# U turned ahead of the first F group, more unread products in TensorE's waits, the last modulation block behind the output products, and branch sums in PSUM

## The chip, the cores and the metric

The kernel is one program for one core of a Trainium2 chip. The metric is the time of a launch on the device in microseconds (us). Engines are named as in the profile: TensorE (PE, and PEld for its loads of the stationary operand), VectorE (DVE), ScalarE (ACT), GpSimd (POOL), and SyncE (SP), which issues nearly all DMAs. Work is ordered between engines by semaphores: an instruction increments one (`then_inc`), another engine waits for a count (`wait_ge`). The page gives the clock that TensorE was granted in tenths of its full 2.4 GHz; its two levels are 1.2 and 2.4 GHz (0.50 and 1.00).

## The reference, cut to what matters

Two blocks run in series on 256 tokens of width 1024, in float32.

```python
# first block, one layer: an S5 state-space mixer, a squared-ReLU MLP, a gated embedding
h = rmsnorm(x, norm_mix)
bu = einsum('blgh,gph->blgp', h by 64 groups of 16, bb)      # complex, state 64 per group
xs = associative_scan(combine, (a, bu))                      # over the 256 tokens
y = gelu(real(xs, c) + d * h);  a, g = split(y @ w_glu);  x = x + a * sigmoid(g)
x = x + relu(rmsnorm(x) @ mlp_w1) ** 2 @ mlp_w2
x = rmsnorm(x + (p @ ple_w) * sigmoid(rmsnorm(x) @ ple_gate_w))
# second block, two layers, a stream x and a context stream ctx (256 tokens)
mod_x, mod_c = silu(c) @ w_ada + b_ada, silu(c_ctx) @ w_ada + b_ada     # 6 x 1024 each
px, pc = split(modulate(rms_norm(x)) @ w_in), split(modulate(rms_norm(ctx)) @ w_in)
y_four, y_conv = fft mixing @ w_four, depthwise conv + layer norm + silu @ w_conv
y_gqa, y_diff = grouped attention @ w_gqa, differential attention @ w_diff
x = x + g_m * (sum(sigmoid(gate_b) * y_b over the 4 branches) @ w_out)
x = x + g_f * swiglu(modulate(rms_norm(x)))                             # ctx too in layer 0
```

## The kernel before, in words

**Products.** A float32 operand is split into a high and a low part (`xh`/`xl`, `wh`/`wl`), and each product is three matmuls: high by high, low by high, high by low (`gemm_pe`, lines 2597 to 2599). Weights stream through a ring of four slots of 1 MB (`raw`), loaded by SP in the fixed order of a list; SP waits until the slot's last user is done. ScalarE makes the high half (`split_hi`, line 819), GpSimd the low half (line 2584; the first two GLU loads are done by VectorE, `gate_lo`, line 3081), and `w_ready` counts the halves. `wh` and `wl` hold two loads. PSUM is two tensors of four banks: `gb` for GEMMs, `mb` for the rest.

**The head** (the first 126 us) builds the state-space mixer as products over chunks of 8 tokens. TensorE runs, in this order: transposes of the lambdas; 21 products nobody reads (`warm`); the transposes of x; 64 transposes that turn x into U (line 2683, [32 x 128] each, into all of `mb`); two products for the row factors `fac` (2690); 8 transposes of c (2696); 4 of the vectors (2701); `warm(2, 2)`; a loop over 32 pairs of groups (2713 and 2724), with modulation blocks 0 to 3 between; the Toeplitz products (2748, 2775, 2761) and blocks 4 to 9; `warm(7, 1)`; then 8 times `y_products(d)` (2799, 2804), after each a late modulation block or one unread product. The late blocks follow y_products 0, 1, 3 and 6. Then GLU starts, first with three weight halves side by side over the eight operand tiles (`leading`).
VectorE computes the first F group (`f_group(0)`, with `mb[:, 0]` as scratch, hence TensorE's wait on `s_F` ahead of the transposes of U), the inverse norms, U itself (3013: `mb` times `fac`), F groups 1 to 3, part of E, the state scan S, the last part of E, `gate_lo` for GLU's load 0, and a loop over the 8 outputs, each turned out of PSUM (`turn_y`, 3090) and passed through the gelu with ScalarE; `gate_lo(1, 0)` and `gate_lo(1, 1)` are inside this loop, behind d = 1 and 3. ScalarE copies `fac` (2360), the row zero of F group 0, then C (2364, 2365), on which the vector transposes and GpSimd's E wait.
SP issues the first four loads when U is turned (`s_U`), the seven zero fills of the Toeplitz tile behind `s_ct5`, and the seven copies inside it (line 640) ahead of ring load 12. The load of the last late block takes the slot of GLU's load 1, so it waits for `gate_lo(1, 1)`.

**Modulation.** `ada_block(n)` (line 667) multiplies 256 columns of w_ada by silu(c) and silu(c_ctx): 8 products, `x16` in the trace, as every float32 product is two records.

**A layer** (`layer_pe`, `layer_act`, `layer_dve`) runs in-projections, Fourier mixing, branch 0, grouped attention, branch 2, diff attention, branches 1 and 3, the out-projection (`wo`), a norm and the feed-forward. Layer 0 has 512 tokens, layer 1 has 256. A branch has four pairs of 256 columns: a gate GEMM, for which ScalarE takes a tanh, and a branch GEMM. VectorE forms `prod = (tanh + 1) * product` (line 2165) and adds it into `mix` in SBUF (2167 to 2171). For branch 3 the result is halved and split again: high by ScalarE (`mixed_hi`, 1832), low by VectorE (`mixed_lo`, 2148), the operands of `wo`.
In the attention loops (`grouped_pe`, `diff_pe`) TensorE issues the scores of item i (1197 to 1201), the transposes of the probabilities of item i - 2 (1208), and the outputs of item i - 3.

**Norms.** `norm_pe` sums squares, and while VectorE forms the inverse root it runs modulation blocks and `unused_products`, products of 256 columns that nobody reads. Norm 7 is that of layer 1's feed-forward.

## Time and profile before

| | us |
|---|---|
| three runs | 1982.76, 1982.89, 1986.4; median 1982.89 |
| the profiled execution | 1981.52 |
| its span, first to last instruction | 1979.7 |
| TensorE busy | 1906.8 |
| GpSimd, VectorE, ScalarE busy | 1108.2, 932.6, 756.2 |
| DMA: bytes from HBM, share of 16 engines | 266.70 MB, 43.1% (queue q1) |
| mean granted clock of TensorE | 0.981 |

The page has the sums; where a stage waits is read from the views by time: stretches (busy time and clock of each engine in a window), the timeline (instructions in order, in brackets how long the engine was idle before and what released it), and the chain of waits. A matmul's duration in the timeline overlaps its neighbours'; for a run of them take the next start less the first.

### The profile page before, as it was taken

To read this page: it belongs to the slowest core of one execution; us is meant where nothing else is said; L and a number is where in the kernel's file an instruction comes from. 1 tells how busy PE (TensorE), PEld (TensorE's weight loads), DVE (VectorE), ACT (ScalarE), POOL (GpSimd) and SP (SyncE) were. 2 spreads that over 40 slices of the span, in tenths; PEclk is the share of its full clock that TensorE was granted. 3 is DMA by queue.
4 is the path that set the end of the run, shared out by engine and by line. 5 is a ranking of instruction groups with operands and counts; after the bars stand their busy time and mean duration, and the time that the engine had idled before them with its cause. 6 is when DMAs were issued, how large, how long until landed. Compare 5 with 4: busy or idle time off the path is not lost.

```text
span 1979.7 us, 31484 instructions
## 1 busy us (share of the span) xinstructions
PE 1906.8 (96%) x13077; PEld 1639.1 (83%) x13077; DVE 932.6 (47%) x1688; ACT 756.2 (38%) x1212; POOL 1108.2 (56%) x611
## 2 busy tenths in 40 slices
PE   8989999989999999999999999999999998989997
PEld 5578999877887788778878888888788987989997
DVE  7956542254935793752443111114476756382112
ACT  4343553333234523642323222222345536434443
POOL 6426898563535443334543444444368754868885
PEclk8989999989999999999999999999999999999999
DMA  6857766764222132114334323223535331665653
GB/s 167 239 200 238 262 216 213 263 202 161 64 74 86 33 123 69 33 65 138 107 109 147 92 84 119 89 75 105 190 125 156 119 106 43 213 227 174 195 168 99
DMA packets 289490, 276.60 MB, mean 140 GB/s; under 512 B 19802, under 2 KB 276324, under 8 KB 289092
## 3 DMA queue, kind: packets, MB, share of 16 engines
q1 hardware_dynamic: 286804, 271.42, 43.1%
q10 hardware_dynamic: 2192, 2.77, 0.5%
q8 instruction: 103, 1.69, 0.4%
q0 software_dynamic: 352, 0.40, 0.1%
q14 instruction: 39, 0.32, 0.0%
HBM read 266.70 MB, written 4.19 MB: 137 GB/s over the span
## 4 chain that ended last, share of the span: by engine, by line
PE 88%; DVE 5%; ACT 2%; DMA 2%; issue 1%; SPq 1%; POOL 1%; ACTq 0%; DVEq 0%; POOLq 0%
PE gb L2597 19%; PE gb L2599 19%; PE gb L2598 19%; PE gb L1755 3%; PE gb L1756 3%; PE gb L1754 3%; PE gb L1482 3%; PE gb L1484 3%; PE gb L1483 3%; PE mb L1208 1%; DMA raw<-in_w_ada 1%; PE gb L667 1%; PE mb L667 1%; PE mb L1275 1%; PE mb L1355 1%
## 5 line engine op out<-in xcount | busy, mean ns | idle before, releaser
L2584 POOL TENSOR_TENSOR wl<-raw,wh 128x1024 fp32r<-128x1024 f32 (+3 forms) x448 | 978.2, 2202 | 780.1 <-ACT wh L819 779.8
L819 ACT CAST wh<-raw 128x1024 fp32r<-128x1024 f32 (+3 forms) x452 | 420.2, 938 | 651.8 <-PE gb L2599 375.6
L2597 PE MATMUL gb<-xh,wh 128*128 128x256 f32 (+1 forms) x1856 | 602.5, 325 | 10.6 <-DVE xl L1158 5.3
L2598 PE MATMUL gb<-xl,wh 128*128 128x256 f32 (+1 forms) x1856 | 598.5, 322 | 0.0
L2599 PE MATMUL gb<-xh,wl 128*128 128x256 f32 (+1 forms) x1856 | 598.4, 322 | 0.0
L2597 PEld LDWEIGHTS gb<-xh,wh 128*128 128x128 f32 x1856 | 350.7, 189 | 46.9 <-issue 11.7
L2599 PEld LDWEIGHTS gb<-xh,wl 128*128 128x128 f32 x1856 | 350.7, 189 | 27.5
L2598 PEld LDWEIGHTS gb<-xl,wh 128*128 128x128 f32 x1856 | 350.9, 189 | 27.2
L1754 PE MATMUL gb<-fhh,wh 128*128 128x512 f32 (+1 forms) x352 | 118.4, 336 | 0.0
L1756 PE MATMUL gb<-fhh,wl 128*128 128x512 f32 (+1 forms) x352 | 117.9, 335 | 0.0
L1755 PE MATMUL gb<-fhl,wh 128*128 128x512 f32 (+1 forms) x352 | 117.9, 335 | 0.0
L1482 PE MATMUL gb<-wh,xh 128*128 128x512 f32 x272 | 107.5, 395 | 0.0
L2261 DVE SCALAR_TENSOR_TENSOR x<-gb,mod,x 128x256 f32<-128x256 f32 x72 | 31.9, 480 | 160.1 <-PE gb L1756 136.9
L1483 PE MATMUL gb<-wh,xl 128*128 128x512 f32 x272 | 105.9, 390 | 0.0
L1484 PE MATMUL gb<-wl,xh 128*128 128x512 f32 x272 | 105.9, 389 | 0.0
L2285 DVE SCALAR_TENSOR_TENSOR pr<-th,gb 128x1024 f32<-128x1024 f32 (+1 forms) x22 | 21.0, 955 | 138.2 <-ACT th L1890 138.2
L2599 PE MATMUL gb<-brh,wl 128*128 128x512 f32 (+1 forms) x256 | 85.8, 335 | 0.0
L2597 PE MATMUL gb<-brh,wh 128*128 128x512 f32 (+1 forms) x256 | 85.8, 335 | 0.0
L2598 PE MATMUL gb<-brl,wh 128*128 128x512 f32 (+1 forms) x256 | 85.7, 335 | 0.0
L2290 DVE TENSOR_TENSOR pr<-pr,gb 128x1024 f32<-128x1024 f32 (+1 forms) x22 | 21.0, 955 | 135.9 <-PE gb L2599 135.9
L2084 DVE SCALAR_TENSOR_TENSOR mb<-upad,vecs,mb 128x256 f32<-128x256 f32 (+1 forms) x152 | 79.5, 605 | 0.0
L867 ACT ACTIVATE th<-gb 128x512 f32<-128x512 f32 (+1 forms) x44 | 34.1, 774 | 115.7 <-PE gb L2599 115.7
(475 smaller groups left out, 3020.2 us busy)
## 6 DMA issues: line engine op xcount, KB each, us to landing
raw<-in_w_in SPq DMA_DIRECT2D x62, 1024.0 KB, 5.3
raw<-in_w_ada SPq DMA_DIRECT2D x48, 1024.0 KB, 5.5
raw<-in_w_ffn SPq DMA_DIRECT2D x44, 1024.0 KB, 5.2
raw<-in_mlp_w SPq DMA_DIRECT2D x32, 1024.0 KB, 5.6
raw<-in_w_ffn SPq DMA_DIRECT2D x16, 768.0 KB, 4.3
raw<-in_w_ffn SPq DMA_DIRECT2D x16, 640.0 KB, 4.1
raw<-in_ssm_w_glu SPq DMA_DIRECT2D x8, 1024.0 KB, 7.1
raw<-in_w_out SPq DMA_DIRECT2D x8, 1024.0 KB, 4.8
```

Source lines behind the costliest of these rows:

```text
L819: nc.scalar.copy(split_half(wh, p, j, h), raw_half(p, it, j, h)).then_inc(hi_ready, 1)
L1482: nc.tensor.matmul(g, xh[:, k, ts], H[:, kk], start=(k == 0), stop=False)
L1483: nc.tensor.matmul(g, xl[:, k, ts], H[:, kk], start=False, stop=False)
L1484: ins = nc.tensor.matmul(g, xh[:, k, ts], L[:, kk], start=False, stop=(k == KD - 1))
L1754: nc.tensor.matmul(o, H[:, kk, :], XH, start=(k == 0), stop=False)
L1755: nc.tensor.matmul(o, H[:, kk, :], XL, start=False, stop=False)
L1756: ins = nc.tensor.matmul(o, L[:, kk, :], XH, start=False, stop=(k == kt - 1))
L2084: D1.add(v.scalar_tensor_tensor(dst, u, w, src, ALU.mult, ALU.add))
L2584: nc.gpsimd.tensor_tensor(split_half(wl, p, j, h), raw_half(p, it, j, h), split_half(wh, p, j, h).bitcast(F32), ALU.subtract)\
L2597: nc.tensor.matmul(o, H[:, k, :], XH, start=st, stop=False)
L2598: nc.tensor.matmul(o, H[:, k, :], XL, start=False, stop=False)
L2599: return nc.tensor.matmul(o, L[:, k, :], XH, start=False, stop=sp_)
```

## The change

In the head, TensorE turns groups 16 to 63 of U before it waits for the first F group, and groups 0 to 15 after it. The 8 transposes of c move ahead of the two products for `fac`; ScalarE copies C before `fac` and row zero. `warm(7, 1)` becomes `warm(13, 1)`. The late modulation blocks follow y_products 0, 1, 3 and 7; behind the one at index 6 there is an unread product instead.
`unused_products` takes a place. Three stand behind the first scores of the grouped heads, four behind the third of the diff heads (both layers), and norm 7 has seven in place of two.
The products of branch 3 and their final sums with `mix` go to `mb` (`mixed_pair`), two banks per pair of tiles, and both splits read them there; VectorE waits on `s_ml` for the splits of two pairs before it reuses a bank. Branches 0 to 2, the running sums and the norm tiles stay in SBUF.

```diff
-        def unused_products(n):
+        def unused_products(n, place=None):
             for _ in range(n):
-                nc.tensor.matmul(gb[:, 2, 0:2 * P], ones[:, :], ...
+                nc.tensor.matmul(gb[:, 2, 0:2 * P] if place is None else place, ones[:, :], ...
@@ norm_pe
-                unused_products(2 if n == 7 else 1)
+                unused_products(7 if n == 7 else 1)
@@ grouped_pe, for i, ahead of the scores
+                    if i == 1:
+                        if c0 >= 4:
+                            pe.wait_ge(s_ex, c0 - 3)
+                        unused_products(3, gb[:, c0 % 4, 0:2 * P])
@@ diff_pe, behind the scores
                 if i == 2:
                     pe.wait_ge(s_qtl, TN[l, "d"] + 8)
                     pe.wait_ge(s_qv, l + 1)
+                    unused_products(4, mb[:, mine[0] % 2, 0:2 * P])
@@ layer_act, mixed_hi
-                    nc.scalar.mul((brh if k < 4 else xh)[:, k, home("layer", T)], mix[:, k, 0:T], 0.5).then_inc(s_mh, 1)
+                    nc.scalar.mul((brh if k < 4 else xh)[:, k, home("layer", T)], mixed_pair(l, k // 2)[:, k % 2, :], 0.5)\
+                        .then_inc(s_mh, 1)
+        def mixed_pair(l, pair):
+            return mb[:, 2 * (pair % 2):2 * (pair % 2) + 2, 0:layer_T(l)]
@@ layer_dve, mixed_lo
-                    v.scalar_tensor_tensor(lo[:, k, home("layer", T)], mix[:, k, 0:T], 0.5, ...
+                    v.scalar_tensor_tensor(lo[:, k, home("layer", T)], mixed_pair(l, k // 2)[:, k % 2, :], 0.5, ...
@@ branch_dve
+                        if b == 3 and pair > 1:
+                            dve.wait_ge(s_ml, 8 * l + 2 * (pair - 1))
-                        prod = dst if b == 0 else two(pr2, s_, T)
+                        prod = dst if b == 0 else mixed_pair(l, pair) if b == 3 else two(pr2, s_, T)
                         if b == 3:
-                            v.tensor_tensor(dst, dst, prod, ALU.add).then_inc(s_mx, 1)
+                            v.tensor_tensor(prod, dst, prod, ALU.add).then_inc(s_mx, 1)
@@ ScalarE, head: the copy of fac and f_row_zero(0) move behind the two copies of C
-            act.wait_ge(s_fp5, 1)
-            nc.scalar.copy(fac[:, :], gb[:, 3, 0:NCH]).then_inc(s_fac, 1)
-            f_row_zero(0)
             act.wait_ge(s_ct5, 1)
...
+            act.wait_ge(s_fp5, 1)
+            nc.scalar.copy(fac[:, :], gb[:, 3, 0:NCH]).then_inc(s_fac, 1)
+            f_row_zero(0)
@@ TensorE, head: and the two products for fac (s_fp5) move behind the transposes of c (s_ct5)
-            pe.wait_ge(s_F, 1)
             pe.wait_ge(s_xg, CH)
-            for g in range(GROUPS):
+            for g in (*range(16, GROUPS), *range(16)):
+                if g == 0:
+                    pe.wait_ge(s_F, 1)
...
-            warm(7, 1)
+            warm(13, 1)
...
-                late = ((0,), (1,), (), (2,), (), (), (3,), ())[d]
+                late = ((0,), (1,), (), (2,), (), (), (), (3,))[d]
```

## Rows read from the trace of the kernel before

**Rows 1.** The page, head and part 1: busy us (share of span) x instructions.

```profile
span 1979.7 us, 31484 instructions
...
PE 1906.8 (96%) x13077; PEld 1639.1 (83%) x13077; DVE 932.6 (47%) x1688; ACT 756.2 (38%) x1212; POOL 1108.2 (56%) x611
```

**Rows 2.** Stretches of 10 us: length, busy (instructions) per engine, granted clock, DMA share, GB/s.

```profile
20.00:30.00 10.00, 6.72 (x30) 3.76 (x29) 9.33 (x20) 8.69 (x10) 7.67 (x9) 0.94 0.48 145
30.00:40.00 10.00, 9.47 (x75) 9.00 (x74) 4.08 (x14) 1.08 (x5) 0.00 (x0) 0.50 0.22 69
100.00:110.00 10.00, 8.21 (x177) 5.20 (x178) 5.08 (x8) 3.69 (x7) 0.00 (x0) 0.66 0.91 316
820.00:830.00 10.00, 9.48 (x62) 7.60 (x60) 7.57 (x15) 7.32 (x21) 4.08 (x8) 0.83 0.00 1
1730.00:1740.00 10.00, 8.18 (x65) 7.98 (x64) 9.96 (x6) 4.19 (x7) 9.24 (x5) 0.95 0.68 231
1740.00:1750.00 10.00, 8.81 (x66) 8.60 (x65) 6.81 (x7) 3.80 (x7) 5.56 (x3) 0.88 0.42 129
```

**Rows 3.** Timeline of TensorE in the head: start, us, operation, [idle before it <- releaser].

```profile
29.72 7.00 PE L2683 MATMUL mb<-const,xg 32*128 32x32 f32 x64 [2.94 <-issue]
...
37.52 1.95 PE L2696 MATMUL gb<-const,cnat 128*128 128x128 f32 x8
...
41.61 3.62 PE L2669 MATMUL gb<-ones 128*128 128x512 f32 x4
...
88.89 6.28 PE L2669 MATMUL gb<-ones 128*128 128x512 f32 x14
101.59 1.08 PE L2799 MATMUL mb<-toep,U 128*32 128x128 f32 x16 [6.42 <-issue]
```

**Rows 4.** Timeline of ScalarE and VectorE in the head.

```profile
38.00 2.29 DVE L3013 TENSOR_TENSOR U<-mb,fac 128x2048 f32<-128x2048 f32 x1 [5.54 <-ACT fac L2360]
...
39.98 0.60 ACT L2365 ACTIVATE Ct<-gb 128x512 f32<-128x512 f32 x1
...
99.70 2.36 DVE L3081 TENSOR_TENSOR wl<-raw,wh 128x1024 fp32r<-128x1024 f32 x2 [0.22 <-DVE E L3000]
...
107.82 0.66 DVE L3090 STREAM_TRANSPOSE gl<-mb 128x256 f32<-128x256 f32 x1 [2.38 <-PE mb L2804]
```

**Rows 5.** Timeline of SP's queue, the Toeplitz copies.

```profile
87.71 6.56 SPq L640 DMA_DIRECT2D toep<-toep  x7
```

**Rows 6.** Chain of waits, 24 to 130 us: start, us, what.

```profile
94.32 9.64 DMA raw<-in_w_ada
...
117.24 5.01 DMA raw<-in_w_ada
```

**Rows 7.** Timeline of TensorE at the last modulation block.

```profile
122.29 1.94 PE L667 MATMUL gb<-raw,sc 128*32 128x256 f32 x16 [3.09 <-DMA raw<-in_w_ada]
...
126.11 0.58 PE L2597 MATMUL gb<-xh,wh 128*128 128x256 f32 x1
```

**Rows 8.** Timeline of TensorE, diff heads of layer 0, third item.

```profile
818.60 0.63 PE L1208 MATMUL mb<-const,probs 128*128 128x128 f32 x4 [2.41 <-DVE probs L1415]
```

**Rows 9.** Timeline of layer 1's mixer end: VectorE, GpSimd, TensorE.

```profile
1729.77 7.75 DVE L2148 SCALAR_TENSOR_TENSOR brl<-mix,brh 128x256 fp32r<-128x256 f32 x4 [5.99 <-ACT brh L1832]
...
1737.99 2.36 POOL L2584 TENSOR_TENSOR wl<-raw,wh 128x1024 fp32r<-128x1024 f32 x1 [0.76 <-ACT wh L819]
...
1738.17 0.39 PE L2597 MATMUL gb<-dqTh,wh 128*128 128x256 f32 x1 [1.82 <-DVE pr L2165]
...
1748.21 0.39 PE L2597 MATMUL gb<-xh,wh 128*128 128x256 f32 x1 [1.19 <-DVE xl L2148]
```

**Rows 10.** Line 2148: count, duration ns min/median/max, first and last start, forms.

```profile
L2148 DVE SCALAR_TENSOR_TENSOR xl<-mix,xh x8: 414/689/2890, 981.2 to 1748.1; 128x512 fp32r<-128x512 f32 x4, 128x256 fp32r<-128x256 f32 x4
```

**Rows 11.** Timeline of TensorE behind norm 7.

```profile
1776.04 0.36 PE L2597 MATMUL gb<-xh,wh 128*128 128x256 f32 x1 [0.95 <-DVE xl L1158]
...
1778.46 0.38 PE L2597 MATMUL gb<-xh,wh 128*128 128x256 f32 x1 [1.12 <-DVE xl L1158]
```

More of the change, by code:

```diff
@@ L941, in first_norm_pe @@
             unused_products(2)
-        def unused_products(n):
+        def unused_products(n, place=None):
             for _ in range(n):
-                nc.tensor.matmul(gb[:, 2, 0:2 * P], ones[:, :], ones[:, :].unsqueeze(1).to_broadcast([P, 2, P]),
+                nc.tensor.matmul(gb[:, 2, 0:2 * P] if place is None else place, ones[:, :], ones[:, :].unsqueeze(1).to_broadcast([P, 2, P]),
                                  start=True, stop=True)
@@ L2147, in mixed_lo @@
                     hi, lo = (brh, brl) if k < 4 else (xh, xl)
-                    v.scalar_tensor_tensor(lo[:, k, home("layer", T)], mix[:, k, 0:T], 0.5, hi[:, k, home("layer", T)].bitcast(F32),
+                    v.scalar_tensor_tensor(lo[:, k, home("layer", T)], mixed_pair(l, k // 2)[:, k % 2, :], 0.5,
+                                           hi[:, k, home("layer", T)].bitcast(F32),
                                            ALU.mult, ALU.subtract)\
@@ L2686, in _ @@
             pe.wait_ge(s_x1, 1)
-            pe.wait_ge(s_small, 32)
-            pe.wait_ge(s_chk, 1)
-            for a in range(2):
-                ins = nc.tensor.matmul(gb[:, 3, GH * a:GH * a + GH], const[:, REP:CHK], chk[:, a, :], start=True, stop=True)
-            ins.then_inc(s_fp5, 1)
             pe.wait_ge(s_cnat, 16 * 8)
@@ L2697, in _ @@
             ins.then_inc(s_ct5, 1)
+            pe.wait_ge(s_small, 32)
+            pe.wait_ge(s_chk, 1)
+            for a in range(2):
+                ins = nc.tensor.matmul(gb[:, 3, GH * a:GH * a + GH], const[:, REP:CHK], chk[:, a, :], start=True, stop=True)
+            ins.then_inc(s_fp5, 1)
             pe.wait_ge(s_vnat, 16 * NVEC)
```

## The prediction

> **What bounds the kernel now.** I read the page first: TensorE is busy for 1906.8 us of a span of 1979.7 us [rows 1]. With 96% of the span taken, a change can only gain where TensorE waits, or where it works at its lower clock level. So I went through the span in stretches of 10 us and looked for a granted clock below 1.00 or a busy time well below 10 [rows 2]. The reader is to see three kinds of place. In the head of the kernel (up to 130 us) there are long stretches at the low level: 0.50 in 30:40, 0.66 in 100:110 (and the same in 120:130). In the attention parts there are short dips: 0.83 in 820:830, and two more like it (630:640 at 0.85, 1650:1660 at 0.83). At the end of layer 1's mixer, 1730:1740 and 1740:1750 have both a shorter busy time and a clock of 0.95 and 0.88. The mixer of layer 0 at the same step (960 to 1000 us) has TensorE 10.0 busy at 1.00: nothing to gain there. The timelines of these places [rows 3 to 11] carry the rest.
>
> The profiled execution took 1981.52 us (span 1979.7), 1.4 us less than the median of the three runs, 1982.89. I sum against the profiled execution and add the 1.4 us at the end. A measurement of this kernel can tell some 4 us (0.2%) from no change.
>
> **Part 1: U is turned ahead of the first F group, the c rows ahead of the row factors.** Now the 64 transposes of U begin at 29.72, after 2.94 us of idle time [rows 3], when the first F group is done. That idle time ends the full clock: all of 30:40 runs at 0.50 with TensorE 9.47 of 10 us busy. In the new order 48 of the 64 need no F, and start where the idle time began, at 29.72 - 2.94 = 26.78. Their price at the low level is 7.00 / 64 = 0.109 us; at the full level I take half, 0.055 (an estimate by the two levels). Will the clock hold, now that there is no gap? Row 30:40 has TensorE busy with exactly these transposes, and it does not rise again. So I let it fall about where it fell before (some 28.9: a clock of 0.94 over 20:30 [rows 2] is 1.2 us at 0.50): 2.1 us at 0.055 make 38, ten at 0.109 end at 30.0, and the 16 that wait for F (done at 29.7) end at 31.8. U is turned 4.9 us earlier than 36.7.
>
> Bounds of that: with the clock at full all the way, it ends at 30.6 (6.1 us); with all 48 at the low level, at 26.78 + 5.2 + 1.75 = 33.8 (2.9 us).
>
> The Trainium skill, page "TensorE: Matmul & The Clock Gate", section "Part 4: PE-mode transpose", says that full clock does not set in under transposes, which it does under products. It speaks against a part of this edit: filling the gap with transposes would not keep the clock. The trace agrees in 30:40 (0.50 at 9.47 busy). By the rule the sum is the one that I take; without it, it is the first rival's.
>
> Behind U come the c transposes (1.8 to 1.95 us at low clock [rows 3]): 31.8 to 33.7. Then the row factors' products, ScalarE's copy of them and VectorE's product U: in the trace 38.00 - 36.72 = 1.28 us from the end of U's transposes to VectorE's start [rows 4]. ScalarE now copies C first; its second copy ended at 40.58, 1.1 us behind the c transposes [rows 3, 4], so it is free at 34.8, and fac follows at 35.0. VectorE starts U at 35.15 in place of 38.00: **2.85 us**. VectorE has no pause from there to 102.06 (0.22 us idle before its row at 99.70, and nothing longer in between [rows 4]), so its whole chain, including the last gate_lo, ends 2.85 us earlier, at 99.2.
>
> TensorE gains more. The vector transposes wait for ScalarE's copies of C (34.8), then take 1.1 and the two wide products behind them 3.62 us at low clock [rows 3]: 39.5 in place of 45.2. So the loop over 32 pairs, the Toeplitz products and the early modulation blocks move up by **5.6 us**; it never waited for a load there, and the F groups it needs (2.85 earlier) were ready more than 2.85 us ahead. SP's loads start when U is turned, so SP and the rings move with it, and so do its seven copies into the Toeplitz tile: issued at 87.71 to 94.27 now [rows 5], the last landed when y_products(0) starts, at 101.59 [rows 3]; then 96.0.
>
> **Part 2: warm(13) in place of warm(7).** Seven products took 6.28 us, 0.9 each [rows 3]; thirteen take 11.7. They start at 88.89 - 5.6 = 83.3 and end at 95.0, 1.0 us before y_products(0) can start. So they cost nothing, and the 6.42 us of idle time that preceded the 0.66 of 100:110 shrinks to 1. I take it that the clock holds. If part 1 brought nothing they would end at 100.6, still ahead of 101.59. Now in the y loop: the late block 0 needs a load that landed at 103.96 [rows 6], then 98.35; it takes 1.0 at full clock (half of the 1.94 at low [rows 7]); y_products(1) ends at 100.8. VectorE turns y 0 at 99.2 and y 1 at 100.85, where it did so at 107.82 [rows 4]: **7.0 us** earlier. From y 1 to y 6 VectorE sets the pace (2.5 us each), which stays.
>
> **Part 3: the last modulation block behind y_products(7).** Its load is issued when VectorE has split the second half of a ring slot, at 117.24, and lands at 122.25 [rows 6]; TensorE idles 3.09 us for it, is at the low level afterwards, and y_products(7) and GLU's first product (126.11) stand behind it [rows 7]. With 7.0 us less, the load lands at 115.3. y_products(7) needs VectorE's turn of y 5 only and ends at 114.4; the block runs 115.3 to 116.3; GLU starts at 116.35. Its last operand is ready near 119.5, before TensorE's lead over three weight halves asks for it (about 124), so no new wait. GLU starts 9.8 us earlier, and the 1.7 us that it now runs at half speed (0.58 for the first product) gives 0.8 more. **Head: 10.6 us.** Bounds: 6.5 if the y loop moves only by VectorE's 2.85 us (117.24 - 2.85 + 5.01 + 1.0 = 120.4, so 5.7, and 0.8); 12.6 if the clock holds throughout (rival A).
>
> **Part 4: the sums of branch 3 in PSUM.** In layer 1 VectorE's four splits of brl take 7.75 us beside GpSimd's splits of weights [rows 9]; the same instruction takes 0.41 us at its shortest [rows 10]. They hold back the product at 1737.44, and TensorE waits 1.82 us, until 1738.17; later it waits 1.19 us for xl; and 1730:1750 loses (0.05 + 0.12) x 10 = 1.7 us to the clock. Sum 4.7 us. With mix read from PSUM I price a split at 0.5 us (its nearest rows are 0.41 without and 1.94 in the mean beside GpSimd), four at 2, done before TensorE ends the group at 1736.3. Late next: GpSimd's half of w_out, 1737.99 to 1740.35, which TensorE would then ask for at 1739.1: 1.1 us back. **3.6 us.** Bounds 0 and 4.7. The added wait on s_ml is for VectorE's own splits, finished just before; what is queued behind it is the product of pair 2 or 3, and at worst it is some 0.1 us on VectorE.
>
> The Trainium skill, page "SBUF — State Buffer", section "Who interferes with whom", has a VectorE instruction with two SBUF inputs shut out by a GpSimd instruction that reads SBUF, and one with at most one SBUF input not. The trace agrees with the first half (7.75 us for four of an instruction that can take 0.41); it has no split with mix in PSUM. By the rule the gain is the one above; without it, none.
>
> **Part 5: unread products in the attention and norm 7.** Three of 256 columns (0.45 each, half of the 0.9) behind the first two scores of the grouped heads, four in the diff heads, where TensorE idled 2.41 us [rows 8]: 1.8 us, which fits. The wait ahead of the three is for exponentials long done. They can only bring back the dips: 0.17 x 10 us x 0.95 busy, at most 1.6 us each. Part of that is hidden behind VectorE and ScalarE, and that they always hold the clock isn't shown; I take 0.75 for each of three: **2.2 us** (bounds 0 and 4.8). In norm 7 five more products are 2.25 us. The gap behind them was 0.95 us, and 1.12 us more of waiting follow one operand later [rows 11], together 2.07: cost 0 to 0.2 here, up to 1.3 if the second wait were gone.
>
> **Sum.** 10.6 + 3.6 + 2.2 = 16.4: 1981.52 - 16.4 = 1965.1, and with 1.4 for the median **1966.5 us**.
>
> **Rivals.**
> A. The clock holds through the transposes of U. For it: from 46 to 73 us transposes between short products run at 1.00; against it 30:40. U is turned at 30.6, the c rows at 31.6; with 1.1 and 0.35 for ScalarE VectorE starts at 33.05, 4.9 us earlier than now; that is 2.05 more than in the forecast, and the y loop follows VectorE: head 12.6, time 1964.5.
> B. VectorE remains the bound of the head: the y loop moves by 2.85 us only, because the loads of blocks 0 and 1 share the queues with the Toeplitz copies and don't come earlier. For it: 9.64 us from issue to landing. Against: they are issued behind TensorE's blocks. Head 6.5: 1970.6.
> C. Only the head gains: GpSimd's weights take the place of mix's splits, and the dips return behind the unread products. For it: GpSimd is busy throughout [rows 9]. 1982.9 - 10.6 = 1972.3.
> D. Slower. The two wide products ahead of the loop over pairs fail to raise the clock, because they now come earlier and nothing dense follows. The loop, 28 us at full clock (45 to 73), would then be bound by TensorE at up to twice its time. One round is 0.73 us; all 32 at the low level cost 23 us, and 23 - 16.4 = 7 us more than now: 1989.5. It decides from some 23 slow rounds on. Against it: the first modulation block, 16 products of 256 columns, is behind round 8.
>
> **Chances.** Forecast 0.42, A 0.15, B 0.2, C 0.2, D 0.03. The forecast's own range is 1963 to 1969.5, A lies in it; B and C carry the upper end, and both together would be 6.5 us, 1976.4. Range 1961.5 to 1975. Faster by over 0.2%: 0.93; within 0.2%: 0.04 (B, C and a lost dip elsewhere at once); slower: 0.03.
>
> **What would show it.** In the changed kernel U's transposes start at 26.8 and end near 31.8; VectorE's U starts near 35.2; y_products(0) at 96 with the clock at 1.00 in 90:110; the last block's wait under 1 us and GLU's first product at 116 to 117; near 1715 to 1735 VectorE's splits at 0.5 us and no wait for pr or xl; no dip behind the diff heads' third item. Wrong would be: GLU's start later than 120, or a clock of 0.50 in the pair loop.

## The result, and the profile after

The changed kernel took 1970.55 us (median of five runs, 1965.51 to 1974.19), the kernel before 1982.89 (five runs, 1981.66 to 1986.4). The ratio is 0.9937, with a 95% interval of 0.9916 to 0.9958: faster by 12.3 us, more than the 4 us that count as no change. The forecast was 1966.5 us with a range up to 1975. The profiled execution took 1965.51 us, where the sum had 1965.1; the median lies 5.0 us above it, where I had added 1.4. Of all the times in this document one is of a slow run: e4's sixth, 2687.72 us at a mean granted clock of 0.65; its ratio leaves it out, its median in the table counts it (1971.69 us without it).

All fences of this section are of the changed kernel. First the head and part 1 of its page, beside [rows 1]:

```profile
span 1963.7 us, 31592 instructions
...
PE 1908.0 (97%) x13129; PEld 1639.0 (83%) x13129; DVE 919.7 (47%) x1688; ACT 756.6 (39%) x1212; POOL 1103.0 (56%) x611
```

TensorE has 1.2 us more work in a span that is 16.0 us shorter: what went is waiting and time at the low clock. The stretches of 10 us, with the columns of [rows 2]:

```profile
20.00:30.00 10.00, 9.85 (x79) 6.88 (x77) 9.33 (x20) 8.35 (x10) 7.78 (x9) 0.97 0.47 145
30.00:40.00 10.00, 9.39 (x40) 6.83 (x39) 7.04 (x21) 5.23 (x16) 5.17 (x3) 0.52 0.75 257
90.00:100.00 10.00, 7.42 (x70) 3.50 (x72) 9.38 (x10) 2.51 (x3) 0.00 (x0) 1.00 1.04 281
100.00:110.00 10.00, 9.51 (x244) 5.74 (x232) 6.88 (x15) 5.79 (x11) 0.00 (x0) 1.00 0.50 173
810.00:820.00 10.00, 10.00 (x77) 7.68 (x77) 8.81 (x17) 8.26 (x24) 4.93 (x8) 1.00 0.01 2
1725.00:1735.00 10.00, 8.68 (x73) 8.51 (x72) 4.58 (x9) 4.44 (x6) 7.75 (x4) 1.00 0.59 194
```

The clock of 30:40 is as low as before (0.52; it falls at 29.4 us), while 100:110 (0.66 before), the third item of the differential heads (0.83) and the mixer's end (0.95 and 0.88) are at 1.00. Timeline of TensorE in the head, beside [rows 3] and [rows 7]:

```profile
26.41 3.18 PE L2697 MATMUL mb<-const,xg 32*128 32x32 f32 x48
29.74 1.91 PE L2697 MATMUL mb<-const,xg 32*128 32x32 f32 x16 [0.15 <-DVEq L2997]
...
40.21 0.42 PE L2738 MATMUL mb<-U,w 128*64 128x32 f32 x8 [0.22 <-ACT w L2400]
...
97.41 0.64 PE L2813 MATMUL mb<-toep,U 128*32 128x128 f32 x16 [1.72 <-issue]
...
116.45 1.07 PE L667 MATMUL gb<-raw,sc 128*32 128x256 f32 x16 [0.27 <-DMA raw<-in_w_ada]
117.46 0.39 PE L2610 MATMUL gb<-xh,wh 128*128 128x256 f32 x1
```

U is turned from 26.41 on, without the 2.94 us of idle time. GLU's first product starts at 117.46, where it started at 126.11: 8.65 us earlier, and its block's wait is 0.27 us in place of 3.09. Timeline of VectorE in the head, beside [rows 4]:

```profile
34.85 2.29 DVE L3027 TENSOR_TENSOR U<-mb,fac 128x2048 f32<-128x2048 f32 x1 [2.32 <-ACT fac L2377]
...
101.99 0.66 DVE L3104 STREAM_TRANSPOSE gl<-mb 128x256 f32<-128x256 f32 x1 [1.23 <-PE mb L2818]
```

And the chain of waits there, beside [rows 6] (start, us, what; DVEq is VectorE's sequencer):

```profile
61.64 0.03 DVEq L2997
...
77.89 3.71 PE mb L2775 x32
...
83.08 0.59 SPq L640
...
89.91 9.67 DMA raw<-in_w_ada
...
111.37 5.04 DMA raw<-in_w_ada
```

Before, the chain ran along TensorE from 46 us to the copies of [rows 5]. Now it follows VectorE's F groups up to 61.64: the loop over pairs starts 5.9 us earlier, but takes 28.2 us (40.21 to 68.45) in place of 27.0 (46.12 to 73.15), so the copies are issued only 4.63 us earlier (83.08 against 87.71).

The mixer's end of layer 1, VectorE, TensorE and GpSimd, beside [rows 9]:

```profile
1715.85 4.92 POOL L2597 TENSOR_TENSOR wl<-raw,wh 128x1024 fp32r<-128x1024 f32 x3 [0.90 <-ACT wh L819]
1716.16 1.42 DVE L2158 SCALAR_TENSOR_TENSOR brl<-mb,brh 128x256 fp32r<-128x256 f32 x4 [6.17 <-ACT brh L1837]
...
1726.91 0.36 PE L2610 MATMUL gb<-brh,wh 128*128 128x256 f32 x1 [1.32 <-issue]
```

Four splits take 1.42 us (7.75 before), with GpSimd busy beside all of them. The Trainium skill, page "SBUF — State Buffer", section "Who interferes with whom", says that a VectorE instruction with at most one SBUF input, outside the modes that use both port pairs, isn't shut out by GpSimd. The trace agrees: 0.36 us for each split with mix in PSUM (the four overlap a little), 1.94 with both inputs in SBUF. TensorE waits once there, for 1.32 us, where it waited for 1.82 and 1.19.

The differential heads of layer 0, beside [rows 8], and norm 7, beside [rows 11]:

```profile
807.87 1.99 PE L946 MATMUL mb<-ones 128*128 128x256 f32 x8 [1.53 <-DVE brl L1731]
809.70 0.60 PE L1208 MATMUL mb<-const,probs 128*128 128x128 f32 x4
```

```profile
1757.48 3.19 PE L946 MATMUL gb<-ones 128*128 128x256 f32 x14
1760.31 0.47 PE L2610 MATMUL gb<-xh,wh 128*128 128x256 f32 x1
...
1762.44 0.38 PE L2610 MATMUL gb<-xh,wh 128*128 128x256 f32 x1 [0.71 <-DVE xl L1158]
```

**Where the 16 us of the two profiled executions came from.** The start of the same product in both traces, after minus before:

| where | before | shift, us |
|---|---|---|
| GLU's first product | 126.11 | -8.65 |
| ahead of the grouped heads of layer 0 | 435.25 | -9.34 |
| diff heads of layer 0, third item | 818.60 | -8.90 |
| same, two items later | 823.91 | -10.97 |
| behind the norm after layer 0's mixer | 1039.43 | -12.04 |
| first products of layer 1 | 1415.22 | -13.08 |
| diff heads of layer 1, fourth item | 1653.21 | -13.41 |
| mixer's end of layer 1 | 1748.21 | -16.91 |
| behind norm 7 | 1776.04 | -15.72 |

The head gives 8.65 + 0.7, the attentions some 1.9 (0.5, 1.1 and 0.3), the sums 3.5. At norm 7 some 1 us is lost again (see e8). The 2.1 us between 824 and 1415 lie where nothing was changed: the kernel before had low stretches at 1032.4 us (3.4 us long) and at 1404.5 (6.8), the changed one had none at the first place and 3.4 us at the second. The experiments show how much of that is chance.

### The profile page after: what moved, and what is told of

It is laid out like the page before. It is cut to its first block, busy times and chain, and to the rows that moved or that the text cites. A ratio compares the mean times of both kernels' runs of the same rounds, so it can differ in the third digit from the quotient of the medians.

```text
span 1963.7 us, 31592 instructions
## 1 busy us (share of the span) xinstructions
PE 1908.0 (97%) x13129; PEld 1639.0 (83%) x13129; DVE 919.7 (47%) x1688; ACT 756.6 (39%) x1212; POOL 1103.0 (56%) x611
## 4 chain that ended last, share of the span: by engine, by line
PE 87%; DVE 7%; ACT 2%; issue 2%; DMA 1%; POOL 1%; SPq 1%; ACTq 0%; DVEq 0%; POOLq 0%
PE gb L2610 19%; PE gb L2611 19%; PE gb L2612 19%; PE gb L1761 3%; PE gb L1759 3%; PE gb L1760 3%; PE gb L1487 3%; PE gb L1489 3%; PE gb L1488 3%; PE mb L1208 1%; PE mb L667 1%; PE gb L667 1%; DMA raw<-in_w_ada 1%; PE mb L1275 1%; DVE mx L1237 1%
## 5 line engine op out<-in xcount | busy, mean ns | idle before, releaser
L867 ACT ACTIVATE th<-gb 128x512 f32<-128x512 f32 (+1 forms) x44 | 34.1, 774 | 115.8 <-PE gb L2612 115.8
```

## The experiments

Each ran beside the kernel before, four kernels to a chip, 5 to 12 runs each. An interval is 0.1 to 0.2%, 2 to 4 us, to each side, so a single median doesn't tell 2 us. I therefore also count, in the profiled execution of each, the stretches at the low clock. "Low" is their sum from GLU's first product to the last product, in brackets how many begin there; before, e6, e9 and e10 also have the end of one that began ahead of it. "Rest" is the time between those two less half of low (TensorE works at half speed there, if it has work). A kernel that loses stretches which cost less than half their length therefore shows a longer rest, as e10 does. Times in us.

| kernel | median | ratio, interval | GLU's first product | low (stretches) | rest |
|---|---|---|---|---|---|
| before | 1982.89 | | 126.11 | 35.9 (8) | 1825.0 |
| changed | 1970.55 | 0.9937, 0.9916 to 0.9958 | 117.46 | 17.1 (4) | 1827.1 |
| e1 changed, again | 1973.19 | 0.9949, 0.9928 to 0.9969 | 119.82 | 30.7 (5) | 1827.2 |
| e2 head alone | 1977.58 | 0.9965, 0.9954 to 0.9977 | 119.48 | 41.0 (9) | 1825.4 |
| e3 without the sums | 1975.45 | 0.9956, 0.9944 to 0.9968 | 118.52 | 37.5 (7) | 1825.7 |
| e4 without attention products | 1972.27 | 0.9939, 0.9920 to 0.9958 | 121.91 | 27.3 (7) | 1824.9 |
| e5 U behind F | 1976.64 | 0.9968, 0.9955 to 0.9982 | 127.49 | 34.1 (8) | 1824.8 |
| e6 late block at 6 | 1970.67 | 0.9950, 0.9931 to 0.9969 | 124.32 | 32.3 (6) | 1826.8 |
| e7 diff products early | 1970.51 | 0.9944, 0.9929 to 0.9960 | 118.97 | 20.5 (4) | 1827.0 |
| e8 same, norm 7 with two | 1973.68 | 0.9951, 0.9936 to 0.9967 | 119.40 | 34.1 (6) | 1824.8 |
| e9 sums alone | 1978.05 | 0.9967, 0.9956 to 0.9979 | 124.78 | 35.5 (8) | 1820.0 |
| e10 unread products alone | 1980.86 | 0.9991, 0.9980 to 1.0001 | 127.18 | 28.3 (6) | 1829.2 |
| e11 head and sums | 1972.71 | 0.9943, 0.9931 to 0.9956 | 119.90 | 34.1 (8) | 1823.3 |
| e12 seven warming pairs | 1972.44 | 0.9943, 0.9930 to 0.9955 | 120.14 | 27.3 (6) | 1824.9 |

The kernel before had a median of 1984.24 beside e1 to e4, 1983.06 beside e5 to e8, 1983.46 beside e9 to e12.

**e1: the changed kernel once more.** No edit.

> The changed kernel once more, as the yardstick of the three beside it. Its five times lay between 1965.51 and 1974.19 us, and the profiled one (span 1963.7) had only five stretches at the low clock against eleven before. Theory: the place of a few low-clock stretches differs from execution to execution, so the five times here lie again within 1965 to 1975 with a median near 1970, and a profile whose time is some us longer shows one to three more stretches at 0.50 in the windows, with the waits unchanged. Rival: the spread comes from elsewhere (a DMA, a wait that differs), then a longer profile has a longer wait and no more low-clock stretches.

1973.19 us, with five of the six times in the expected 1965 to 1975 and one far outside (1984.28), and a profiled span of 1973.0 us where the first was 1963.7. The same program, compared product by product, is 2.4 us later at GLU and 9.3 us later at the end. In the profile of e1:

```profile
100.00:110.00 10.00, 8.20 (x183) 4.93 (x178) 5.10 (x11) 3.78 (x8) 0.00 (x0) 0.83 0.47 164
...
1020.00:1030.00 10.00, 9.89 (x79) 7.23 (x72) 4.23 (x19) 3.05 (x3) 3.00 (x2) 0.66 0.42 124
...
1640.00:1650.00 10.00, 8.32 (x44) 6.14 (x42) 7.11 (x16) 6.10 (x17) 3.69 (x6) 0.83 0.02 7
```

The clock is at 1.00 in the changed kernel's first trace in all three. Behind GLU's start the two executions differ by 6.95 us, and half of the difference in low is (30.7 - 17.1) / 2 = 6.8: the low stretches are all of it, and the rest is equal to 0.1 us. Over all 11 runs of the changed kernel the mean granted clock goes from 0.979 (1984.28 us) to 0.992 (1965.51 us), with 1.4 us for each 0.001 and a correlation of -0.97. In the 48 runs of the kernel before beside the experiments it goes from 0.977 to 0.985, with 1.2 us for each 0.001. Pooled, the means are 1972.3 and 1983.2 us: the change is worth about 10.9 us, not 16.0.

**e2: the head alone** (parts 1 to 3 on the kernel before; the U, c and fac order, warm(13), the late block).

```
+            pe.wait_ge(s_xg, CH)
+            for g in (*range(16, GROUPS), *range(16)):
...
-            warm(7, 1)
+            warm(13, 1)
...
-                late = ((0,), (1,), (), (2,), (), (), (3,), ())[d]
+                late = ((0,), (1,), (), (2,), (), (), (), (3,))[d]
```

> The kernel before with the edits of the head alone: U turned ahead of the first F group, c ahead of fac on TensorE and ScalarE, warm(13, 1), last modulation block behind y_products(7). Theory (the head gives 9.5 us of the 16.0 in the trace): GLU's first product at 117.5 us, times 9 to 10 us below before, 1973.5 us. Rival (the head's gain is given back later by a load that is now late): GLU at 117.5 but under 6 us in the time, and a wait for a load in the first 400 us that the kernel before does not have.

6.9 us (4.6 to 9.1) below before, with GLU's start at 119.48: 6.6 us earlier, where 9 to 10 us and 117.5 were expected. The rival is out: the lead of 7.4 us at 200 us is still there at 780 us, and no wait for a load was added. Behind GLU's start there are nine low stretches, in the kernel before eight and the end of a ninth.

**e3: the changed kernel without the sums** (mix in SBUF again).

```
-    v.tensor_tensor(prod, dst, prod, ALU.add).then_inc(s_mx, 1)
+    v.tensor_tensor(dst, dst, prod, ALU.add).then_inc(s_mx, 1)
```

> The changed kernel with the products and sums of branch 3 back in SBUF (mix and pr2), all else as changed. Theory (GpSimd's splits of weights hold up VectorE's splits that read two SBUF tiles): the four splits of brl in layer 1 take some 7.7 us again in place of 1.4, TensorE waits 1.8 and 1.2 us there, and the time is 3.5 us longer than that of the changed kernel run beside it. Rival (the gain at this place comes from the clock alone): the splits are slow again, but with the clock at 1.00 at this place less than 1.5 us is lost.

0.9956 against the changed kernel's 0.9937 and 0.9949: the sums are worth 1.4 to 3.8 us by the medians. The four splits take 7.75 us again, with waits of 1.8 and 1.2 us behind them, and at this place the trace loses 3.4 us against the changed kernel. It has a low stretch of 3.4 us here too (1732.7), so alone it doesn't part the waits from the clock. e2 and e10 do: with mix in SBUF and the clock at 1.00 over the whole mixer's end they lie, product for product, where the kernel before lies (a shift of 0.03 us from 1735 to 1750 of its time), since the wait for xl takes up what the clock gives. TensorE in e2, where before has 1.19 us:

```profile
1742.18 0.39 PE L2597 MATMUL gb<-xh,wh 128*128 128x256 f32 x1 [2.66 <-DVE xl L2148]
```

So the low stretch cost nothing at this place. All ten profiled executions with the sums in PSUM gain 3.4 to 3.5 us here, the four without them nothing.

**e4: the changed kernel without unread products in the attentions** (norm 7 keeps its seven).

```
-    unused_products(3, gb[:, c0 % 4, 0:2 * P])
...
-    unused_products(4, mb[:, mine[0] % 2, 0:2 * P])
```

> The changed kernel without the unread products in the grouped and in the diff heads (three and four, in both layers). In the trace of the changed kernel the four of the diff heads start 1.53 and 1.27 us late, behind the wait for s_qtl, and the transposes after them come 1.0 us later than before. Theory (they cost 1.0 us per layer and bring back a dip of 1 to 2 us where one falls): the waits for probs at the third diff item are 2.1 to 2.4 us again, up to four dips of the clock return, and the median is 0 to 3 us longer than the changed kernel's. Rival (the products cost more than they bring): the median is 1 to 2 us shorter.

0.9939: nothing lost, and nothing won. Yet the low stretches are back at 623.9, 815.1 and 1644.5 us. In its profile the third item again waits, in front of a stretch of 0.83:

```profile
812.79 0.63 PE L1208 MATMUL mb<-const,probs 128*128 128x128 f32 x4 [2.40 <-DVE probs L1415]
```

**e5: U behind the F group again**, all else as changed.

```
-    pe.wait_ge(s_xg, CH)
-    for g in (*range(16, GROUPS), *range(16)):
-        if g == 0:
-            pe.wait_ge(s_F, 1)
+    pe.wait_ge(s_F, 1)
+    pe.wait_ge(s_xg, CH)
+    for g in range(GROUPS):
```

> The changed kernel with one thing put back: the 32 U transposes wait for the F group again, in order 0 to 31. My theory is that U turned early is what brings the head forward: the pair loop is behind VectorE's F group and U copy, and putting U back makes the GLU's first product 3 to 5 us later than in the changed kernel's profiled execution (117.46 us there), so 120.5 to 122.5, and the time 3 to 5 us above the changed kernel. The rival is that the modulation blocks' transfers bound the head (TensorE waits for their weights at 99.62, 102.34 and 116.45 us in one execution and until 103.6 in the other): then the GLU starts within 1.5 us of the two executions seen (117.5 and 119.8) and the time stays within 1.5 us of the changed kernel's.

(The expectation speaks of 32 transposes; there are 64.) 0.9968: by the ratios 3.8 to 6.1 us above the changed kernel's two medians, as the theory had it. The loop over pairs starts at 46.30, 6.1 us later. But GLU's start at 127.49 is 5 us later than expected, and the profile says why:

```profile
80.00:90.00 10.00, 10.00 (x74) 7.53 (x67) 9.56 (x27) 1.01 (x1) 0.00 (x0) 0.72 0.88 291
90.00:100.00 10.00, 10.00 (x62) 4.73 (x63) 9.51 (x19) 2.96 (x4) 0.00 (x0) 0.76 0.65 155
```

A low stretch of 10.2 us from 84.5 on, with TensorE 10.00 busy, doubles the time of the state products and modulation blocks ahead of SP's copies. Such a stretch is also in e4 (64.1) and e6 (78.1), three of the ten executions with thirteen warming pairs and in none of the four with seven (before, e9, e10, e12). From the loop over pairs to the first output these three take 61.1 to 62.6 us, the changed kernel 57.2. The stretch starts ahead of the warming pairs, which start at 95.3 us here, so they aren't its cause in any way that I can see; it stays open.

**e6: the last modulation block back at index 6.**

```
-    late = ((0,), (1,), (), (2,), (), (), (), (3,))[d]
+    late = ((0,), (1,), (), (2,), (), (), (3,), ())[d]
```

> The changed kernel with the last modulation block back at index 6, ahead of the last y_products. Its weights came at 116.2 us in the changed kernel's profiled execution, so by the theory the last y_products (0.6 and 1.1 us of products, then a copy and a split by VectorE and ScalarE) start behind that wait, at about 117, and the GLU's first product comes at 119 to 120 where it was 117.46: 1.5 to 2.5 us later. The rival is that the earlier pair loop lets SP issue the block's copies earlier still and the wait is gone at either place: then GLU start and time are the changed kernel's within 0.5 us and within the noise.

```profile
102.61 0.65 PE L2813 MATMUL mb<-toep,U 128*32 128x128 f32 x16 [2.21 <-issue]
...
121.45 1.07 PE L667 MATMUL gb<-raw,sc 128*32 128x256 f32 x16 [2.49 <-DMA raw<-in_w_ada]
```

The low stretch at 78.1 makes the whole head late, so I read from the first output product on: 21.71 us to GLU. The three executions that have the block at its new place, and no low stretch in the outputs, take 20.05 (changed), 20.09 (e5) and 21.13 us (e3). The edit is worth 0.6 to 1.7 us, at the lower end of my 1.5 to 2.5; the wait of 2.49 us is back. So is a low stretch behind it, at 122.5: all four profiled executions with the block at index 6 have one at 121 to 125 us (before, e6, e9, e10), none of the ten with it behind y_products(7). The median doesn't show the edit.

**e7: the differential heads' four products ahead of the wait.**

```
     if i == 2:
+        pe.wait_ge(s_qtl, TN[l, "d"] + 5)
+        unused_products(4, mb[:, mine[0] % 2, 0:2 * P])
         pe.wait_ge(s_qtl, TN[l, "d"] + 8)
         pe.wait_ge(s_qv, l + 1)
-        unused_products(4, mb[:, mine[0] % 2, 0:2 * P])
```

> The changed kernel with the four unread products of each differential attention moved ahead of the wait that they stood behind: they now follow the wait for five of the turned tiles and stand ahead of the wait for the eighth. In the changed kernel the third item's transposes come 0.95 and 1.0 us later than before against the product ahead of them, since four products of nearly 2.0 us start when the data is already near. By the theory this comes back, 1.9 us for the two layers, and no low stretch appears in their place: 1 to 2.5 us below the changed kernel. The rival is that the stretch at the high clock behind the third item depends on the products standing where they stand: then a low stretch at about 812 or 1640 us takes it back, and the time is that of the changed kernel or above.

1970.51 us, no gain. The third item does come earlier, but it and the next now wait for VectorE:

```profile
807.64 1.99 PE L946 MATMUL mb<-ones 128*128 128x256 f32 x8
810.12 0.63 PE L1208 MATMUL mb<-const,probs 128*128 128x128 f32 x4 [0.48 <-DVE probs L1421]
...
812.17 0.66 PE L1208 MATMUL mb<-const,probs 128*128 128x128 f32 x4 [0.53 <-DVE probs L1421]
```

Against the changed kernel the shift is 1.39 us ahead of the item, 0.42 at it, 1.05 at the next and 1.00 behind the heads: of the 1.0 us that was won 0.6 is given back, most of it within one item, and 0.4 stays, as in layer 1. So the products cost 0.4 us in each layer and not the 1.0 of my theory; the rest of the delay that the shift table shows at 818.60 was hidden behind VectorE's probabilities. The median can't show so little.

**e8: e7, and norm 7 with two products.**

```
-                unused_products(7 if n == 7 else 1)
+                unused_products(2 if n == 7 else 1)
```

> As the kernel with the diff products moved ahead of the wait, and with norm 7 back at two unread products behind its spreads (seven in the changed kernel). The seven end 0.7 us before the split that the next product needs, and the shift against before falls from 16.9 to 15.7 us there. By the theory they cost 0.8 to 1.2 us and give nothing, so this is 2 to 3.5 us below the changed kernel. The rival is that they hold the clock over the first products of the block behind: then a low stretch at 1754 to 1772 us costs 1 to 2 us and this kernel is no faster than the one before it in this list.

```profile
1765.62 1.03 PE L946 MATMUL gb<-ones 128*128 128x256 f32 x4
1768.30 0.35 PE L2611 MATMUL gb<-xh,wh 128*128 128x256 f32 x1 [1.65 <-DVE xl L1158]
...
1770.72 0.38 PE L2611 MATMUL gb<-xh,wh 128*128 128x256 f32 x1 [1.13 <-DVE xl L1158]
```

From the products' start, the next block's first product comes after 2.68 us and the second operand's after 5.10; in the changed kernel after 2.83 and 4.96. This theory fell too. Nor is the step from -16.91 to -15.72 in the shift table just the changed kernel's low stretch at 1753.2: e1 and e7 have none between 1740 and 1960 us and lose 1.1 and 0.9 us here. What differs is VectorE's first split of xl, another instruction with two SBUF inputs. In e1, and then in e11:

```profile
1767.95 1.34 DVE L1158 SCALAR_TENSOR_TENSOR xl<-sqr,mod,xh 128x256 fp32r<-128x256 f32 x1 [0.61 <-ACT xh L1131]
```

```profile
1766.69 0.48 DVE L1158 SCALAR_TENSOR_TENSOR xl<-sqr,mod,xh 128x256 fp32r<-128x256 f32 x1 [0.18 <-ACT xh L1131]
```

It takes 0.48 to 2.57 us over the fourteen profiled executions, and GpSimd splits weights beside it in all of them, from 1.4 us ahead of the unread products to 0.4 us behind their start. Where GpSimd starts equally early, two and seven unread products give the same time to the second operand: 4.40 us (before, two) and 4.45 (e3, seven) with GpSimd 0.8 us ahead, 5.05 (e2, two) and 5.08 (e12, seven) with 1.2 and 1.3. So five more products cost 0.05 us at most, and the step goes with how VectorE meets GpSimd. What moves GpSimd's start isn't shown.

**e9: the sums alone**, on the kernel before.

```
-    v.tensor_tensor(dst, dst, prod, ALU.add).then_inc(s_mx, 1)
+    v.tensor_tensor(prod, dst, prod, ALU.add).then_inc(s_mx, 1)
```

> The kernel before with only the sums of fused branch 3 moved to PSUM; head, unread products and norm 7 are as before. By the theory the mixer's end is the one stage it touches, and it comes 3.5 us earlier there (the shift table of the changed kernel against before goes from -13.4 to -16.9 us at the mixer's end), so 3 to 4 us below before, ratio 0.998 to 0.9985. The rival is that this step is paid back at once, by a low stretch behind the mixer or by the wait for the block's weights at norm 7: then it is within 1 us of before.

0.9967: 6.5 us (4.2 to 8.7), more than expected. At the mixer's end the shift against before goes from -1.36 to -4.85: 3.5 us, as in the changed kernel. The other 3 us in the profiled execution are not of the edit: 1.4 us in the head and the layers between, and 1.6 us beyond 1800 us (see the last section). For the median, the mean granted clock of its seven runs is 0.9833 beside 0.9808 in the kernel before, 3 us at 1.2 us for each 0.001. That the sums cause this isn't shown; in the profiled pair low is the same (35.5 and 35.9).

**e10: the unread products alone**, on the kernel before.

```
+    unused_products(3, gb[:, c0 % 4, 0:2 * P])
...
+    unused_products(4, mb[:, mine[0] % 2, 0:2 * P])
...
-    unused_products(2 if n == 7 else 1)
+    unused_products(7 if n == 7 else 1)
```

> The kernel before with only the unread products added: three in each grouped attention, four in each differential attention, seven instead of two behind norm 7's spreads. By the theory each group costs TensorE time where it stands (1.0 us in each differential attention, 0.8 to 1.2 us at norm 7, little in the grouped ones, since the wait there was 3 us) and keeps away low stretches that cost 1 to 2 us each and come in only some of the executions: the two cancel, within 1.5 us of before. The rival is the one of the prediction: they give 2.2 us and more, ratio 0.9989 or below, and the low stretches at about 630, 820 and 1650 us are gone.

0.9991: 1.8 us (4.0 below to 0.2 above). The mean granted clock of its 11 runs is 0.9845, that of the kernel before 0.9808; by 1.2 us for 0.001 this would be 4.4 us if low time had one price everywhere. It hasn't: the stretches that go are cheap ones. In the profiled execution those of the first grouped and the first diff heads are gone, for 0.5 and 1.2 us, and the one at 1650 us is still there, now 1.15 us dearer behind the four products. Neither the theory (within 1.5 us) nor the rival (2.2 us and more, all three gone) is met.

**e11: head and sums**, the changed kernel without its added products behind the head.

```
-    unused_products(3, gb[:, c0 % 4, 0:2 * P])
...
-    unused_products(4, mb[:, mine[0] % 2, 0:2 * P])
...
-    unused_products(7 if n == 7 else 1)
+    unused_products(2 if n == 7 else 1)
```

> The changed kernel without any of its added unread products in the attentions and at norm 7 (head and sums alone). By the theory these two hold all of the gain: as fast as the changed kernel or up to 2 us faster, ratio 0.993 to 0.995. The rival is that the products carry a part: then it is 2 us or more above the changed kernel's two medians (ratios 0.9937 and 0.9949), at 0.996 or above.

0.9943, between the two medians of the changed kernel. Head and sums hold the gain.

**e12: seven warming pairs.**

```
-            warm(13, 1)
+            warm(7, 1)
```

> The changed kernel with 7 pairs of unread products instead of 13 ahead of the outputs. In the changed kernel TensorE still waits 1.7 to 2.2 us behind the 13 for the copies of toep to land, so the 6 pairs less (5.2 us) only lengthen that wait to about 7 us. By the theory y_products(0) starts at the same 97.4 us within 0.5, but at the low clock or shortly before it falls, and the outputs with the GLU's first product come 1 to 3 us later. The rival is that the wait was always harmless: the GLU starts at 117.5 to 119.8 us as in the two executions of the changed kernel, and the time is the same within noise.

```profile
90.00:100.00 10.00, 2.77 (x28) 1.20 (x34) 9.49 (x10) 1.99 (x2) 0.00 (x0) 0.83 1.03 247
100.00:110.00 10.00, 10.00 (x238) 6.15 (x242) 6.45 (x12) 3.28 (x8) 0.00 (x0) 0.83 0.62 218
```

And of TensorE's timeline:

```profile
98.83 1.08 PE L2813 MATMUL mb<-toep,U 128*32 128x128 f32 x16 [7.22 <-issue]
```

The wait for the first output grows to 7.22 us, and from the loop over pairs to the first output it is 57.4 us, as in the changed kernel (57.2). A low stretch of 6.8 us is there, as in all four kernels with seven pairs; with thirteen it is absent in four of ten, 3.4 us long in five and 6.8 in one. In time it shows no loss: 0.9943, and 21.31 us from the first output to GLU, where the changed kernel has 20.05 and e1 22.64.

No version beats the changed kernel by more than its interval.

## Why the prediction was right, and where it was off

**Mechanism.** Forecast, and what the traces of the changed kernel have:

| step | forecast | changed | e1 |
|---|---|---|---|
| U's transposes start | 26.8 | 26.41 | 26.28 |
| VectorE's U starts | 35.15 | 34.85 | |
| y_products(0) | 96.0 | 97.41 | 97.18 |
| y 1 turned | 100.85 | 101.99 | |
| GLU's first product | 116.35 | 117.46 | 119.82 |

The transposes kept no clock: it fell at 29.4 us with 48 of them already under way from 26.41, as the Trainium skill's page "TensorE: Matmul & The Clock Gate", section "Part 4: PE-mode transpose", would have it. So rival A is out. The loop over pairs ran at 1.00 in both executions of the changed kernel. Rival D's mechanism shows in small elsewhere: 3.4 us at 0.50 in the loop of e2 and e7, and in e4 the stretch at 64.1 that makes the loop 2.0 us longer (30.2 us in place of 28.2), far from its 23 slow rounds.

**Part 1, mis-sized: 5.6 us at TensorE became 4.2.** I wrote that the F groups "were ready more than 2.85 us ahead". They weren't all: in the loop over pairs TensorE now waits 1.0 us for VectorE, at three places, and 0.5 for ScalarE, and the chain runs through VectorE up to 61.64. VectorE as the bound is rival B's, but not for B's reason: the load that B wanted held back was issued 4.4 us earlier (89.91 in place of 94.32) and took 9.67 us where it had taken 9.64.

**Head: 10.6 forecast, 6.9 (4.6 to 9.1) measured alone.** "I take it that the clock holds" in the outputs was true in the profiled execution (8.65 + 0.7 = 9.4 us) but not in most. GLU's first product came 6.2 to 7.6 us earlier in e1, e2, e3, e7, e8 and e11, and 4.2 in e4. With U put back the median loses 3.8 us or more (e5); the late block is 0.6 to 1.7 us (e6) where its wait promised 3; six more warming pairs show no gain (e12).

**Part 4: 3.6 forecast, 3.4 to 3.5 in all ten traces that have it.** By medians 6.5 us alone and 1.4 to 3.8 taken out of the whole. The split at 0.36 us is below my 0.5. The amount holds, the split into causes doesn't: I counted 1.7 us for the clock beside 1.19 for the wait for xl, and e2 and e10 show one cause, a wait of 2.6 us for VectorE, which a low stretch only fills.

**Part 5: 2.2 forecast for the attentions, less 0 to 0.2 for norm 7; 1.8 (4.0 to -0.2) measured alone, nothing when taken out (e4, e11).** The count of stretches says more than the medians. In the attentions there are 15 low stretches in the five executions without the products there (before, e2, e4, e9, e11) and 6 in the nine with them (none in changed, e7, e8 and e12, one in e1, e3, e6 and e10, two in e5). So there are fewer stretches with the products, two thirds of one in place of three, though they don't always hold. What a stretch of 3.4 us costs there can be read from the shifts: 0.5 us in the first grouped heads; in the diff heads 0.9 to 1.6 without the products, and 1.6 to 1.7, half its length, behind them (e3, e5, e6, e1, e10). The products themselves cost 0.4 us in each diff attention. So a stretch that comes all the same costs more than it did. Over the four attentions together, against the trace of before, the seven executions with the products at their place gain 0.7 us in the mean, the five without them 0.1, and the two with them early (e7, e8) 2.7. The 2.2 was the gain where all three stretches go and none comes, as in the changed kernel's profile and e12 (2.0); in the mean it is some 0.5.

**Sum.** 16.4 forecast, 16.0 in the profiled pair, 10.9 in the means. The terms that were too large are the head (10.6, 6.9 alone) and the attentions (2.2, some 0.5); with 3.5 for the sums they make 10.9. The head was priced as if the clock always held in the outputs, and adding only "1.4 for the median" took one execution for a typical one. It was the fastest of 11, with 17.1 us of low time where e1 had 30.7; before had 35.9. Some 5 us of the agreement at 1965 is luck. Rival C (only the head gains) is out by e9 and e11; its price of 10.6 us was mis-sized with the head.

## What to carry to other kernels

Where the same program's low-clock stretches come and go, one pair of traces tells a stage's waits but not the total: count the stretches in both, put the median against the mean clock of all its runs, and forecast from several executions, not from the profiled one. A stretch at the low clock is worth half its length only where TensorE is the bound (1.6 us of 3.4 at 780 us). Where VectorE sets the pace it was worth 0.5 to 1.7 us in the attentions and nothing at the mixer's end: before a low clock is counted as a loss of its own, ask whether the next wait would end any earlier without it. Where VectorE has two SBUF inputs, look at what GpSimd does beside it. When an engine's start is brought forward by 5 us, check every operand over the whole loop behind it, not only the first rounds.

## What the runs showed of the hardware that was not expected

The stretches at the low clock have a few places where they come in almost every execution of every kernel here (420 to 450, 1020 to 1040 and 1395 to 1409 us, ahead of or in the norms with modulation blocks), and others that come in about half of them (780 us, in seven of fourteen, in part of the kernel that no edit touched; 1.6 us for a stretch of 3.4, 3.2 for one of 6.8). Six runs of one program gave 0.979 to 0.990 in mean clock and 1984.28 to 1969.48 us.

From 1800 to 1950 us TensorE's products follow each other every 118.6 ns in twelve of the fourteen profiled executions and every 117.3 ns in two (e9 and e10, which share no edit and ran on one chip with e11 and e12, which have 118.6), all at a granted clock of 1.00. That is 1% and 1.6 us of span. No run here shows why.
